# Moving three quarters of a small matrix-vector product from TensorE to VectorE inside the merge loop of a hybrid GLA / neighbourhood-attention block

## The reference, cut to what matters

```python
def ada_mod(cond, w, b):
    m = (jax.nn.silu(cond) @ w + b)[:, None, :]
    return jnp.split(m, 6, axis=-1)

sh1, sc1, gt1, sh2, sc2, gt2 = ada_mod(cond, w_ada, b_ada)
h = rmsnorm(x, g_mix) * (1 + sc1) + sh1
...
mix = (jax.nn.sigmoid(m_gla) * b_gla + jax.nn.sigmoid(m_na) * b_na) @ w_out
x = x + gt1 * mix
h2 = rmsnorm(x, g_ffn) * (1 + sc2) + sh2
x = x + gt2 * conv_ffn(h2, w_up, w_conv, b_conv, w_down)
```

## Time and profile before

| | |
|---|---|
| median of three runs | 1007.43 us (1007.32 to 1007.87) |
| the profiled execution, its own time | 1007.67 us |
| its span in the profile | 1005.8 us |
| granted TensorE clock, mean | 0.998 |
| PE busy | 983.5 us, 98% |
| DVE busy | 560.2 us, 56% |
| ACT busy | 434.9 us, 43% |
| POOL busy | 484.4 us, 48% |

### The profile page before, as it was taken

One profiled execution on the slowest core, in us unless ns is written; L12 is line 12 of the kernel. 1 busy time (PEld: TensorE's weight loads), 2 busy tenths in 40 slices (PEclk: granted clock), 3 DMA queues, 4 the chain that ended last, 5 costly groups with the idle time before them and its releaser, 6 DMA issues.

```text
span 1005.8 us, 18390 instructions
## 1 busy us (share of the span) xinstructions
PE 983.5 (98%) x7187; PEld 915.0 (91%) x7187; DVE 560.2 (56%) x1041; ACT 434.9 (43%) x668; POOL 484.4 (48%) x337
## 2 busy tenths in 40 slices
PE   4999999999999999999999999999999999999998
PEld 3999999999788889999988899999999999888886
DVE  7507358964365652322325898777777777913002
ACT  4243264442676664222241455555555556611110
POOL 1475831222342322323243467888888887433231
PEclk9999999999999999999999999999999999999999
DMA  9977222213001114665672122233222231322231
GB/s 340 309 87 102 63 63 64 62 46 84 12 23 42 43 43 154 218 226 163 212 248 87 42 84 75 84 90 91 85 84 85 84 96 53 126 72 75 88 126 58
DMA packets 132066, 105.38 MB, mean 105 GB/s; under 512 B 6902, under 2 KB 112283, under 8 KB 131739
## 3 DMA queue, kind: packets, MB, share of 16 engines
q1 hardware_dynamic: 127112, 97.32, 32.5%
q0 software_dynamic: 1568, 3.15, 2.1%
q10 hardware_dynamic: 3315, 3.94, 1.1%
HBM read 99.91 MB, written 3.42 MB: 103 GB/s over the span
## 4 chain that ended last, share of the span: by engine, by line
PE 91%; DVE 3%; issue 2%; SPq 1%; POOL 1%; DMA 1%; ACT 1%; DVEq 0%; POOLq 0%; ACTq 0%
PE PJ L724 11%; PE PJ L729 10%; PE PJ L725 10%; PE PA L1246 6%; PE PA L1247 6%; PE PA L1248 6%; PE PA L1139 4%; PE PA L1140 4%; PE PA L1141 4%; PE PJ L1139 3%; PE PJ L1141 3%; PE PJ L1140 3%; PE PA L1048 2%; PE PJ L1031 2%; PE PA L862 2%
## 5 line engine op out<-in xcount | busy, mean ns | idle before, releaser
L554 POOL TENSOR_TENSOR wlo<-wraw,whi 128x1024 fp32r<-128x1024 f32 x66 | 165.8, 2513 | 340.4 <-ACT whi L1299 251.7
L724 PE MATMUL PJ<-h_hi,whi 128*128 128x320 f32 x640 | 196.4, 315 | 0.4 <-ACT qk_rs L1454 0.4
L725 PE MATMUL PJ<-h_lo,whi 128*128 128x320 f32 x640 | 192.7, 309 | 0.0
L729 PE MATMUL PJ<-h_hi,wlo 128*128 128x320 f32 x640 | 145.8, 309 | 0.0
L724 PEld LDWEIGHTS PJ<-h_hi,whi 128*128 128x128 f32 x640 | 120.2, 188 | 3.1 <-issue 1.4
L725 PEld LDWEIGHTS PJ<-h_lo,whi 128*128 128x128 f32 x640 | 120.3, 188 | 0.0
L1299 ACT ACTIVATE whi<-wraw 128x1024 fp32r<-128x1024 f32 x51 | 53.7, 1053 | 143.9 <-PE PJ L729 79.1
L729 PEld LDWEIGHTS PJ<-h_hi,wlo 128*128 128x128 f32 x640 | 107.0, 188 | 0.0
L1690 ACT ACTIVATE whi<-wraw 128x1024 fp32r<-128x1024 f32 x21 | 22.3, 1061 | 98.7 <-PE PA L1141 51.6
L681 POOL TENSOR_TENSOR behind<-behind_val,behind 128x512 fp32r<-128x512 f32 x40 | 52.1, 1301 | 19.0 <-ACT behind L1669 19.0
L1248 PE MATMUL PA<-h_hi,behind 128*128 128x320 f32 x192 | 59.3, 309 | 0.0
(11 more groups left out here) (439 smaller groups left out, 2774.7 us busy)
## 6 DMA issues: line engine op xcount, KB each, us to landing
wraw<-in_w_in_dram SPq DMA_DIRECT2D x82, 256.0 KB, 3.1
ada_rest<-in_w_ada_dram SPq DMA_DIRECT2D x32, 512.0 KB, 5.1
wraw<-in_w_up_dram SPq DMA_DIRECT2D x48, 256.0 KB, 3.5
wraw<-in_w_down_dram SPq DMA_DIRECT2D x42, 256.0 KB, 3.1
raw_even<-in_w_up_dram SPq DMA_DIRECT2D x40, 256.0 KB, 3.6
ada<-in_w_ada_dram SPq DMA_DIRECT2D x8, 1024.0 KB, 9.6
out_dram<-x ACTq DMA_DIRECT2D x10, 256.0 KB, 2.5
x_rows<-in_x_sample_dram SPq DMA_DIRECT2D x2, 1024.0 KB, 7.0
```

Of the source, the lines that this page charges most:

```text
L554: pool.tensor_tensor(wlo[:, slot, 0:k, :], wraw[:, slot, 0:k, :], whi[:, slot, 0:k, :].bitcast(F32), ALU.subtract).then_inc(lo_done, 1)
L724: pe.matmul(out, whi[:, slot, w0 + k, :], hi(k)[:, tok], start=start and k == k0, stop=False)
L725: pe.matmul(out, whi[:, slot, w0 + k, :], lo(k)[:, tok], start=False, stop=False)
L729: mm = pe.matmul(out, wlo[:, slot, w0 + k, :], hi(k)[:, tok], start=False, stop=stop and k == k1 - 1)
```

## The change

VectorE takes six of the eight contraction blocks of `rest`. For pieces `a` = 0, 1, 2 (blocks k = 0 to 5) and for each of the two conditions `v`, it multiplies `ada_rest` (128 x 512) by the condition's value of each partition and adds up: two `tensor_scalar` and ten `scalar_tensor_tensor` per block of 128 channels, into `rest_sum` (function `weighted`). TensorE then multiplies only piece 3 (k = 6, 7) as before, and sums `rest_sum` over the partitions by a stationary `rest_pick`, 32 columns of which one is ones for each `v`: 8 + 8 instructions in place of 32. SP waits for `sum_step` before it reloads pieces 0 to 2.

The order changes with it. In block 0, `rest` comes after the whole attention branch. In blocks 1 to 7, the turn of the previous block's rows into columns comes after the gate projection, and `rest` comes between the GLA and the attention branch. On VectorE the loop body is taken apart into `gated_branch`, `rest_kept`, `modulated_rest`, `weighted` and `attended_branch`.

```diff
             def merge_loads(j, last=False):
-                for h in range(2):
-                    sp.wait_ge(ada2_used, j * 2 + (h + 1))
-                    for a in (2 * h, 2 * h + 1):
-                        ada_rest_piece(a, j * 512 + (ADA_FIRST + 4) * P)
+                for a in range(4):
+                    if a < N_SUMMED:
+                        sp.wait_ge(sum_step, j * SUM_STEPS + 4 * (a + 1))
+                    else:
+                        sp.wait_ge(ada2_used, j + 1)
+                    ada_rest_piece(a, j * 512 + (ADA_FIRST + 4) * P)
...
-            def rest(at, h):
-                for a in (2 * h, 2 * h + 1):
+            def rest(at):
+                for a in range(N_SUMMED, 4):
                     pe.wait_ge(ada_in[a], at(16, 32 + 16))
                     for k in (2 * a, 2 * a + 1):
                         for g in range(4):
-                            mm = pe.matmul(PA[32 * g:32 * g + 32, 1024:1024 + P], cond_rest[:, k, :],
-                                           ada_rest[:, a, k % 2, g * P:(g + 1) * P], start=k == 0, stop=k == NK - 1)
+                            pe.matmul(PA[32 * g:32 * g + 32, 1024:1024 + P], cond_rest[:, k, :],
+                                      ada_rest[:, a, k % 2, g * P:(g + 1) * P], start=k == 2 * N_SUMMED, stop=False)
+                pe.wait_ge(sum_step, at(SUM_STEPS, SUM_STEPS))
+                for v in range(2):
+                    for g in range(4):
+                        mm = pe.matmul(PA[32 * g:32 * g + 32, 1024:1024 + P], rest_pick[:, v, :],
+                                       rest_sum[:, v, g * P:(g + 1) * P], start=False, stop=v == 1)
                 mm.then_inc(ada2_used, 1)
...
+            gla_branch(lambda m, c: c)
+            pe.wait_ge(on_lo, 4)
+            attended(0, 4)
+            pe.wait_ge(cond_again, 5)
+            pe.wait_ge(ko_cp, 1)
+            rest(lambda m, c: c)
+
+            def merge(at):
+
+                pe.wait_ge(sn_set, at(1, 0))
+                project(1, at(2, C_POST + 1), hh, hl, PJ, 0, done=mna_ps)
+                columns(at)
+                pe.wait_ge(t1_set, at(1, 0))
+                gla_branch(at)
+                pe.wait_ge(ada2_rows, at(1, 0))
+                rest(at)
+                pe.wait_ge(ada2_cp, at(1, 0))
+                pe.wait_ge(t2_set, at(1, 0))
+                attended(0, 4)
+
             with pe.Fori(0, NK - 1) as j:
                 merge(lambda m, c: j * m + (m + c))
+            columns(lambda m, c: NK * m + c)
...
+            def weighted(at):
+                for a in range(N_SUMMED):
+                    dve.wait_ge(ada_in[a], at(16, 32 + 16))
+                    for k in (2 * a, 2 * a + 1):
+                        for v in range(2):
+                            scale, out = cond2[:, k, v:v + 1], rest_sum[:, v, :]
+                            if k == 0:
+                                dve.tensor_scalar(out, ada_rest[:, a, k % 2, :], scale, None, ALU.mult).then_inc(sum_step, 1)
+                            else:
+                                dve.wait_ge(sum_step, at(SUM_STEPS, 2 * k + v - 1))
+                                dve.scalar_tensor_tensor(out=out, in0=ada_rest[:, a, k % 2, :], scalar=scale, in1=out,
+                                                         op0=ALU.mult, op1=ALU.add).then_inc(sum_step, 1)
...
+            def rest_kept(j):
+                dve.wait_ge(ada2_used, j + 1)
...
+            def modulated_rest(j, at_):
+                dve.wait_ge(ada2_ps, j + 1)
...
+            dve.wait_ge(ada_in[0], 32 + 16)
+            dve.memset(rest_pick[:, :, :], 0.0).then_inc(cond_again, 1)
+            dve.wait_ge(cond_again, 3)
+            for v in range(2):
+                dve.memset(rest_pick[:, v, v:v + 1], 1.0).then_inc(cond_again, 1)
+            weighted(lambda m, c: c)
+            gated_branch(0)
+            attended_branch(0)
+            rest_kept(0)
+            weighted(lambda m, c: m + c)
+            with dve.Fori(0, NK - 2) as i:
+                gated_branch(i + 1)
+                rest_kept(i + 1)
+                modulated_rest(i, lambda first: bass.ds(i * 4 + first, 4))
+                weighted(lambda m, c: i * m + (2 * m + c))
+                attended_branch(i + 1)
+            gated_branch(NK - 1)
+            rest_kept(NK - 1)
+            modulated_rest(NK - 2, lambda first: slice(4 * (NK - 2) + first, 4 * (NK - 2) + first + 4))
+            attended_branch(NK - 1)
+            modulated_rest(NK - 1, lambda first: slice(4 * (NK - 1) + first, 4 * (NK - 1) + first + 4))
```

More of the change, by code:

```diff
@@ L94 @@
 N_ASIDE = 4
+N_SUMMED = 3
+SUM_STEPS = 4 * N_SUMMED
 GATE_K = [(0, 0, 3), (0, 3, 5), (0, 5, 8), (1, 0, 4), (1, 4, 8)]
@@ L202, in hybrid_dit_step @@
         rest_rows = at("rest_rows", R + 66048, [P])
+        rest_sum = at("rest_sum", R + 128096, [2, 4 * P])
+        rest_pick = at("rest_pick", R + 132192, [2, 32])
         sn = at("sn", R + 57344, [TOK])
@@ L514, in _ @@
                     sp.wait_ge(t1_set, NK)
+                    sp.wait_ge(ada2_used, NK)
                     sp.wait_ge(ko_stored, 16)
@@ L1086, in rest @@
                         for g in range(4):
-                            mm = pe.matmul(PA[32 * g:32 * g + 32, 1024:1024 + P], cond_rest[:, k, :],
-                                           ada_rest[:, a, k % 2, g * P:(g + 1) * P], start=k == 0, stop=k == NK - 1)
-                mm.then_inc(ada2_used, 1)
[L1091 to L1104, removed]
-                project(0, at(2, C_POST + 2), lambda k: og_hi[:, k, :], lambda k: og_lo[:, k, :], PJ, 1, k1=4, done=bg_ps)
[L1106 to L1130, removed]
@@ new lines, in rest, with columns, attended @@
+                mm.then_inc(ada2_used, 1)
+            def columns(at):
+                pe.wait_ge(ada2_rows, at(1, 0))
+                pe.matmul(PA[:, 1536:1544].rearrange("p (a c) -> p a c", c=2), rest_rows[:, :],
+                          ident[:, :].rearrange("p (a r) -> p a r", a=4)[:, :, 0:2], start=True, stop=True).then_inc(ada2_ps, 1)
+            def attended(k0, k1):
+                project(0, None, lambda k: ona_hi[:, k, :], lambda k: ona_lo[:, k, :], PA, 0, k0=k0, k1=k1, w0=4,
+                        start=k0 == 0, stop=k1 == 4, done=bn_ps if k1 == 4 else None)
@@ new lines, in gla_branch @@
+            def gla_branch(at):
+                project(0, at(2, C_POST + 2), lambda k: og_hi[:, k, :], lambda k: og_lo[:, k, :], PJ, 1, k1=4, done=bg_ps)
+            project(1, C_POST + 1, hh, hl, PJ, 0, k1=3, stop=False)
+            values(19)
+            project(1, None, hh, hl, PJ, 0, k0=3, start=False, done=mna_ps)
+            pe.wait_ge(og_lod, 4)
+            pe.wait_ge(pt_cp, 20)
+            gla_branch(lambda m, c: c)
+            pe.wait_ge(on_lo, 4)
+            attended(0, 4)
+            pe.wait_ge(cond_again, 5)
@@ L1568, in _ @@
             act.wait_ge(mixlo_set, NK)
+            act.wait_ge(ada2_ps, NK)
             for n in range(2, 8):
@@ L2090, in _, with one_row, gated_branch @@
             dve.memset(rows_all[:, :, :], 0.0).then_inc(rows_zero, 1)
[L2092 to L2098, removed]
+            def weighted(at):
[10 more added lines that the diff above has]
+                                                         op0=ALU.mult, op1=ALU.add).then_inc(sum_step, 1)
+            def one_row(j):
+                return slice(j, j + 1) if isinstance(j, int) else bass.ds(j, 1)
+            def gated_branch(j):
                 dve.wait_ge(mixlo_set, j)
@@ L2114, in _ @@
                 dve.wait_ge(mixhi_set, j + 1)
-                dve.tensor_tensor(mix_lo[:, bass.ds(j, 1), :], t1[:, :].unsqueeze(1),
-                                  mix_hi[:, bass.ds(j, 1), :].bitcast(F32), ALU.subtract).then_inc(mixlo_set, 1)
+                dve.tensor_tensor(mix_lo[:, one_row(j), :], t1[:, :].unsqueeze(1),
+                                  mix_hi[:, one_row(j), :].bitcast(F32), ALU.subtract).then_inc(mixlo_set, 1)
+            dve.wait_ge(ada_in[0], 32 + 16)
[19 more added lines that the diff above has]
+            modulated_rest(NK - 1, lambda first: slice(4 * (NK - 1) + first, 4 * (NK - 1) + first + 4))
             dve.wait_ge(mixlo_set, NK)
```

16 lines of the change are left out of this document (11 added, 5 removed).

## The result

The changed kernel takes 1013.91 us (median of 5 runs, 1012.9 to 1013.98), the kernel before 1007.87 in the same comparison (1007.32 to 1009.3): ratio 1.0055, with a 95% interval of 1.0044 to 1.0066. It is slower by 0.55%, which is 5.5 us by the ratio and 6.0 by the medians. The forecast was 1015.0, with a range of 1009 to 1021. Its sign, its place and its main mechanism were right. Its three terms were each too high, by 2.6 us in all, and 1.6 us outside the merge stage, of which it says nothing, brought the total back near the forecast.

The account below looks back on a forecast made before the run. TensorE, busy 98% of the span, was taken to bound the kernel. 1007.67 us + 3.9 (block 0) + 2.6 (block 1) + 0.8 (blocks 2 to 7) = 1015.0 us, range 1009 to 1021.

Parts of the forecast that it names:

- three terms: Merge stage: +3.9 us for block 0, +2.6 for block 1, +0.8 for blocks 2 to 7.
- What is removed: TensorE's `rest`: 16 instructions per block instead of 32, 0.94 us gained per block, 7.5 us over 8 blocks.
- Handover behind rest: Blocks 1 to 7: attention branch waits for `mod` until G+1.84 (G: GLA branch's end), leaving 0 of 0.94 us.
- Length of the products: VectorE's twelve added instructions per block take 7.5 us, between 6.5 and 8.4; POOL's `wlo` comes on top.
- Block 0: Uncovered products, stretched by two `wlo` of 2.4 us each, end at 404.1; TensorE waits, block 1 starts +3.9 us.
- rival D: First two blocks: only one of three collisions of products and `wlo` happens, +2 to +4 us, 1010.5; chance 0.13.
- Block 1: Products, stretched 2.4 us by the slot-1 `wlo`, make TensorE wait 2.6 us; block 2 starts +6.5 us.
- the fall itself: Block 0's gap can lower TensorE's granted clock to 0.50, slowing block 1's first 3 us by 1.5 us.
- Blocks 2 to 7: Late `wlo` use up VectorE's room until its round of 16.8 us counts against 16.38: +0.8 us, between 0 and 3.
- A: Rival: POOL and VectorE don't get in each other's way here; 1007.1 us, no change; chance 0.12.
- B: Rival: handover behind `rest` costs half, TensorE gains 0.5 us per block from block 2 on; 1004 us; chance 0.08.
- C: Rival: VectorE and POOL together bound every block, +1.3 us for each of six; near 1023.8, half 1019; chance 0.20.

Follow-up runs that it names:

- e3: The changed kernel without VectorE's weighting and summing (contraction blocks 0 to 5 of `rest` left out), handover waits kept: 1007.93 us, ratio 0.9999.
- e1: The changed kernel with VectorE's copy of the previous block's `mod` moved ahead of the next block's branches: 1009.05 us, ratio 1.0011.
- e5: The changed kernel with the edits of e1 and e2 together, nothing else: 1003.70 us, ratio 0.9961 to the kernel before.
- e4: The changed kernel with 64 more matmuls on TensorE in block 0's gap, their result overwritten: 1011.11 us, ratio 1.0031.
- e7: The changed kernel with POOL's `wlo` in the merge stage in four instructions of 128x256 instead of one of 128x1024: 1011.00 us, ratio 1.0038.
- e2: The changed kernel with block 0's `rest` done wholly on TensorE, VectorE's products beginning with block 1: 1008.94 us, ratio 1.0009.

## Why the prediction was right, and where it was not

**What is removed: right.** `rest` has 256 instructions in the profile, 128 on piece 3 and 128 on the sums. It takes 1.06 us in block 1 (417.17 to 418.23), where 0.94 was forecast.

**Handover behind rest: right.** Forecast G+1.84 for the attention branch and no gain; measured G+1.81 in block 1, and seven waits of 0.8 us in the mean (5.6 in all). That it fits so closely is in part luck: `rest` took 0.12 us longer than forecast, and the way over VectorE 0.75 instead of 0.90. e3 shows it without the products, e1 and e5 take it away and get up to 0.88 us a block back.

**Length of the products: right.** Forecast 0.40 and 0.67 apart, 7.5 us in all; measured 7.5 (408.43 to 415.93 in block 1). The lower end that I kept, 6.5, was worked out wrongly: 2 x 0.40 + 10 x 0.64 is 7.2. The Trainium skill (VectorE: DVE Perf Modes, "The DRAIN you can't avoid") says that the next operation waits for the empty pipeline, and adds, which the prediction left out, that one that isn't held starts earlier. The products are 0.74 long and start 0.66 apart, so they agree with the addition.

**Block 0: mechanism right, size 0.9 too large.** Products until 404.1 were forecast, 403.2 is measured (403.96 less 0.74). Both collisions were there, but the start was 0.3 sooner than forecast (392.21 less 0.74, against 391.8), and each collision cost 2.1 to 2.2 us and not 2.4 (2.90 and 2.83 less 0.74). The earlier trace rows had already shown the smaller price: two POOL instructions made 12.59 out of 8.2 us, 2.2 each. That the second one happened hung on the last product: in e4 and e7 the `wlo` came behind it. So these two kernels had one collision of the three forecast, which is rival D's case, and the changed kernel had two.

**Block 1: the step failed.** The forecast had the slot-1 `wlo` interrupt the products of block 1 and TensorE wait 2.6 us for them. In the trace they run their 6.71 us undisturbed, POOL waits instead (`wlo` 3.50 long), and TensorE doesn't wait for the products at all. What made block 1 longer was the term that I had put at nothing: "TensorE waits 2.6 us for the products in block 1 anyway, so the sum stays". There was no such wait for the low clock to hide in, so its 1.6 us counted in full. Block 2 starts at 422.77 - 0.74 = 422.03, +4.6 instead of +6.5. The forecast of the fall itself was right. The Trainium skill (TensorE: Matmul & The Clock Gate, "What's actually happening") says that an idle engine's clock is halved until activity returns; the gap of 4.0 us shows it, while the gap of 1.8 us in e7 was followed by no fall.

**Blocks 2 to 7: forecast +0.8, measured +0.1.** The distance stays at 16.37 to 16.38, but for one of 16.5. The round of VectorE that I worked out as 16.8 is 16.1 in e1 and e5. It was 0.7 too high because I let the two `wlo` cost 2.4 and some 2; they cost 2.2 (8.86 less 6.71) and 1.5 (2.36 less 0.88).

**The sum.** Forecast 3.9 + 2.6 + 0.8 = 7.3 us on top of 1007.67. Measured in the profiles: 3.0 + 1.6 + 0.1 = 4.7 in the merge stage, and 0.74 + 0.85 outside. By the merge stage alone the forecast was 2.6 too high; it met the total more nearly because of 1.6 us that it doesn't speak of. That part of the agreement is luck. Whether the 0.85 behind the stage belong to the change is open: the same wait of 0.8 us for `wlo` stands in e2, and in none of the other experiments.

**The rivals.** A (no collisions) is refuted by block 0, B (saving kept) by the handover, C (VectorE and POOL bound every block) by e3 and by the distance of 16.38; C is true of e5, at 16.1 us. D is true of e4 and e7, not of the changed kernel.

## What to carry to other kernels

When work is taken off the bounding engine, list first what stands behind the shortened piece in that engine's order and what it waits for: here some 0.9 us of saving stood in front of a chain of three small instructions that was just as long, and putting one copy ahead of the others gave most of it back. Moved work needs cover from its first round on, so the first block deserves a rule of its own. And a gap on TensorE has to be charged with the slow instructions behind it, unless a wait that is really there covers them.

## What the runs showed of the hardware

- Which of VectorE and POOL waits was not what I had read from the earlier trace rows. In a row of back-to-back products POOL sometimes gets in behind the running one (block 0: a product of 2.90 us, `wlo` 3.00) and sometimes not until the row is over: in block 3 the `wlo` issued at 440.40 lasts 5.41 us instead of 2.41, while ten products take their undisturbed 6.71. The Trainium skill (SBUF — State Buffer, "Who interferes with whom") says that the port pair that VectorE shares with GpSimd is an exclusive lock, and that issue order decides who blocks. That fits each single collision; by it alone POOL would have had its turn in block 3 behind the product that was running, and it hadn't. Which of the two happens goes with the time of arrival: in the profiles of the changed kernel, e1, e2, e4 and e5 all 22 `wlo` that came up to 3.4 us behind the start of a row of ten products got in, and of the 14 that came 3.4 to 5.5 us behind it 12 waited for the end of the row. The forecast had the one of block 1 come 4.2 us behind the start; it came 5.5. Two came 3.7 us behind it and got in (e2), so the time alone doesn't settle it; what decides is open.
- An idle time of TensorE of 4.0 us was followed by a granted clock of 0.50 and a loss of 1.6 us; one of 1.8 us was followed by none (e7).
- A handover from TensorE over three small VectorE instructions and back takes 0.75 us (418.23 to 418.98) in the chain.
